# First layer's attention: one maximum over both maps, exponentials read from the PSUM bank, undivided maps joined, outputs by query

## The reference, cut to what matters

```python
def diff_attend(q, k, v, lam):
    s = jnp.einsum('bqhmd,bkhmd->bhmqk', q, k).astype(jnp.float32) * ATTN_SCALE
    p = jax.nn.softmax(s, axis=-1)
    w = (p[:, :, 0] - lam * p[:, :, 1]).astype(v.dtype)
    return jnp.einsum('bhqk,bkhe->bqhe', w, v)
...
def finish(o):
    B, T = o.shape[:2]
    o = rms_norm(o, subln_g) * (1.0 - lam_init)
    return o.reshape(B, T, D_MODEL) @ w_o
```

## Time and profile before

| | us |
|---|---|
| median of 3 runs | 2743.91 |
| lowest and highest run | 2741.31, 2743.94 |
| span of the profiled execution | 2737.2 |
| median less span | 6.7 |

### The profile page before, as it was taken

How to read it: one execution, slowest core, us unless ns; L and a number is a source line. 1 busy time by engine, 2 the same in 40 slices (tenths; PEclk the granted TensorE clock), 3 DMA queues, 4 the chain that set the end, 5 groups by cost and what they waited for, 6 DMA issues and landing times.

```text
span 2737.2 us, 44768 instructions
## 1 busy us (share of the span) xinstructions
PE 2592.4 (95%) x18413; PEld 2330.1 (85%) x18413; DVE 1729.9 (63%) x3255; ACT 1260.2 (46%) x2246; POOL 174.2 (6%) x211
## 2 busy tenths in 40 slices
PE   6999989999989989999999999999999999999998
PEld 4676567888868679999999879899999998798998
DVE  4665946454565566677654877676676558776764
ACT  3444634223255554454444455554544444555543
POOL 1000000000034320000000010000000000100001
PEclk8999999999989999999999999999999999999999
DMA  8655522322325325456555324466765553244653
GB/s 258 209 175 185 186 92 78 104 96 93 100 78 120 88 79 170 166 166 178 165 174 171 123 85 151 129 177 169 201 182 162 171 180 109 85 158 128 175 167 122
DMA packets 515818, 397.02 MB, mean 145 GB/s; under 512 B 26024, under 2 KB 491184, under 8 KB 515616
## 3 DMA queue, kind: packets, MB, share of 16 engines
q1 hardware_dynamic: 512816, 388.02, 46.6%
q0 software_dynamic: 2080, 3.53, 1.0%
q10 hardware_dynamic: 720, 2.62, 0.3%
HBM read 393.08 MB, written 1.05 MB: 144 GB/s over the span
## 4 chain that ended last, share of the span: by engine, by line
PE 81%; DVE 12%; ACT 3%; issue 2%; DMA 1%; POOL 1%; SPq 0%; DVEq 0%; ACTq 0%
PE pv L747 42%; PE pa L747 30%; PE pv L712 4%; DVE Wl L1848 3%; PE pa L712 3%; ACT Wh L1362 1%; PE pa L871 1%; DMA ring<-in_w_mod_dram 1%; PE pa L717 1%; DVE Lb L2000 1%; POOL Pb L2490 1%; DVE T L1921 0%; DVE HTl L1855 0%; DVE T L1920 0%; DVE Pb L2013 0%
## 5 line engine op out<-in xcount | busy, mean ns | idle before, releaser
L1848 DVE TENSOR_TENSOR Wl<-ring,Wh 128x1024 fp32r<-128x1024 f32 (+4 forms) x688 | 760.7, 1147 | 320.2 <-ACT Wh L1362 317.3
L1362 ACT ACTIVATE Wh<-ring 128x1024 fp32r<-128x1024 f32 (+4 forms) x688 | 647.9, 990 | 451.1 <-PE pv L747 446.3
L747 PE MATMUL pa<-HTl,Wh 128*128 128x256 f32 (+2 forms) x1648 | 535.7, 325 | 41.7 <-DVE HTl L1940 23.9
L747 PE MATMUL pv<-HTl,Wh 128*128 128x256 f32 (+1 forms) x1872 | 546.8, 292 | 17.2 <-DVE Wl L1848 5.5
L747 PE MATMUL pv<-HTh,Wl 128*128 128x256 f32 (+1 forms) x1872 | 538.5, 288 | 0.0
L747 PE MATMUL pv<-HTh,Wh 128*128 128x256 f32 (+1 forms) x1872 | 538.0, 287 | 0.0
L747 PE MATMUL pa<-HTh,Wl 128*128 128x256 f32 (+2 forms) x1648 | 521.2, 316 | 0.0
L747 PE MATMUL pa<-HTh,Wh 128*128 128x256 f32 (+2 forms) x1648 | 520.7, 316 | 0.0
L747 PEld LDWEIGHTS pv<-HTl,Wh 128*128 128x128 f32 x1872 | 359.8, 192 | 32.5 <-issue 8.3
L747 PEld LDWEIGHTS pa<-HTl,Wh 128*128 128x128 f32 (+1 forms) x1648 | 320.3, 194 | 77.1 <-issue 43.6
L747 PEld LDWEIGHTS pv<-HTh,Wl 128*128 128x128 f32 x1872 | 360.2, 192 | 2.9 <-issue 0.2
(11 more groups left out here) (237 smaller groups left out, 3836.4 us busy)
## 6 DMA issues: line engine op xcount, KB each, us to landing
ring<-in_ffn_w_gu_dram SPq DMA_DIRECT2D x176, 512.0 KB, 5.1
ring<-in_w_mlp_dram SPq DMA_DIRECT2D x64, 1024.0 KB, 5.3
ring<-in_w_in_dram SPq DMA_DIRECT2D x54, 1024.0 KB, 5.0
ring<-in_w_mod_dram SPq DMA_DIRECT2D x48, 1024.0 KB, 5.9
ring<-in_ffn_w_down_dram SPq DMA_DIRECT2D x64, 704.0 KB, 4.7
ring<-in_a_w_qkv_dram SPq DMA_DIRECT2D x12, 1024.0 KB, 5.3
ring<-in_b_w_qkv_dram SPq DMA_DIRECT2D x12, 1024.0 KB, 5.2
ring<-in_w_out_dram SPq DMA_DIRECT2D x8, 1024.0 KB, 5.1
```

The costliest lines, as they stand in the source:

```text
L747: m = nc.tensor.matmul(o, lhsT=x, rhs=y, start=first and j == 0, stop=last and j == 2)
L1362: ins = nc.scalar.activation(Wh[rows, p % SPLIT, a:b], ring[rows, i % RING, a:b], ACT.Copy)
L1848: ins = v.tensor_tensor(Wl[rows, p % SPLIT, a:b], ring[rows, i % RING, a:b], Wh[rows, p % SPLIT, a:b].bitcast(F32), ALU.subtract)
```

## The change

The first layer's loop becomes a function of its own on PE, ACT and DVE.

- Scores: the two maps of a unit lie in two adjacent banks (`pairs_`). One `tensor_reduce` on DVE takes the negated maxima of both (`nm`, two numbers a row); ACT reads the exponentials straight from the banks, and no copy to `Lb` is made. The banks come free when ACT is done with them.
- Join: with row sums l1 and l2, DVE forms c = -lambda l1 / l2 from two operations on one number a row, then e1 + c e2 in one pass. The pass that scaled the first map is gone; the outputs are too large by l1.
- Outputs: the transposed map is now the stationary operand, so that queries lie on the partitions; they use one fixed bank (`O_BANK`) and `A` rotates over two. ACT takes the mean square of each unit by a Square over 128 columns with a sum. Mean, root and Newton step then work on 4 numbers a row for each head, the epsilon times l1 squared.
- POOL multiplies the head's 128 by 512 outputs by their roots; PE transposes them (4 transposes, `OT`); ACT writes `HTh` from the bank with the gain, and DVE writes `HTl` from it.

```diff
-        pv = [ctx.enter_context(nc.psum_tensor(f"pv{i}", [P, 512], F32)) for i in range(BANKS)]
+        pairs_ = [ctx.enter_context(nc.psum_tensor(f"pv{i}", [P, 2, 512], F32)) for i in range(BANKS // 2)]
+        pv = [pairs_[i // 2][:, i % 2, :] for i in range(BANKS)]
+        O_BANK = pa[BANKS - 2]
...
+            def diff_attention(tag, todo, behind):
+                A.width = 2
+                V.even()
...
+                def outputs_turned(i):
+                    h = last_unit(i, 9)
+                    if h is not None:
+                        pe.wait_ge(on_ready, h + 1)
+                        if A.taken():
+                            pe.wait_ge(a_free, A.taken())
+                        b = A.take((tag, "OT", h))
+                        for t in range(4):
+                            turn(b[:, t * P:(t + 1) * P], Oa[:, h, t * P:(t + 1) * P], a_full if t == 3 else None)
...
+                        h, t, n = todo[i]
+                        for m in range(2):
+                            r = slice(m * HEAD, (m + 1) * HEAD)
                             if V.taken():
                                 pe.wait_ge(v_free, V.taken())
-                            b = V.take((tag, "S", i, m))
+                            mm(V.take((tag, "S", i, m))[:, 0:n], Qa[r, h, t * P:(t + 1) * P], Ka[r, h, 0:n], True, True, v_full)
+                            V.emptied_otherwise((tag, "S", i, m))
...
+                    if i >= 3:
+                        u = i - 3
+                        h, t, n = todo[u]
+                        pe.wait_ge(a_free, A.nth((tag, "T", u)))
+                        if u:
+                            pe.wait_ge(o_free, u)
+                        for k in range(n // P):
+                            mm(O_BANK[:, 0:P], PT[:, u % 2, k * P:(k + 1) * P], Va[:, k, h * P:(h + 1) * P],
+                               k == 0, k == n // P - 1, o_full if k == n // P - 1 else None)
+                    outputs_turned(i)
+                behind(len(todo) + 2)
...
+                def rest_turned():
+                    for i in range(len(todo) + 3, HEAD_NORM_STEPS + 3):
+                        outputs_turned(i)
+                return rest_turned
...
                     src = ht(ALL)
-                    def last_sums(k):
+                    def head_done(k):
                         if k == 4:
-                            for step_ in range(len(todo) + 3, HEAD_NORM_STEPS):
-                                head_sums(step_)
+                            rest_turned()
...
+            def diff_attention(tag, todo, also):
+                for i in range(HEAD_NORM_STEPS + 3):
+                    if i < len(todo):
+                        h, t, n = todo[i]
+                        act.wait_ge(mx_ready, i + 1)
+                        for m in range(2):
+                            nc.scalar.activation(Pb[:, i % 3 * 2 + m, 0:n], V.taken_at((tag, "S", i, m))[:, 0:n], ACT.Exp,
+                                                 bias=nm[:, i % 2, m:m + 1], scale=1.0,
+                                                 accum_out=lsum[:, h % 3, m, t:t + 1]).then_inc(v_free, 1)
...
+                    if 0 <= i - 2 < len(todo):
+                        u = i - 2
+                        n = todo[u][2]
+                        if u >= 1 and last_unit(i - 1, 9) is not None:
+                            act.wait_ge(a_free, A.nth((tag, "OT", last_unit(i - 1, 9))))
+                        copy((tag, "T", u), PT[:, u % 2, 0:n], lambda b: b[:, 0:n])
+                    if 0 <= i - 4 < len(todo):
+                        u = i - 4
+                        h, t, _ = todo[u]
+                        act.wait_ge(o_free, u + 1)
+                        if u >= 2:
+                            act.wait_ge(os_ready, u - 1)
+                        nc.scalar.activation(SQ[:, u % 2, 0:P], Oa[:, h, t * P:(t + 1) * P], ACT.Square,
+                                             accum_out=osum[:, h % 3, t:t + 1]).then_inc(os_ready, 1)
+                    h = last_unit(i, 6)
+                    if h is not None:
+                        act.wait_ge(om_ready, h + 1)
+                        x = oroot[:, h % 2, :]
+                        nc.scalar.activation(x, omean[:, h % 2, :], ACT.Ln).then_inc(log_ready, 1)
+                        act.wait_ge(log_ready, seen.more(log_ready))
+                        nc.scalar.activation(x, x, ACT.Exp, scale=-0.5).then_inc(or_ready, 1)
+                    h = last_unit(i, 9)
+                    if h is not None:
+                        act.wait_ge(a_full, A.nth((tag, "OT", h)))
+                        b = A.bank((tag, "OT", h))
+                        nc.scalar.activation(HTh[:, h, :], b[:, 0:512], ACT.Copy, scale=gq[:, 4:5]).then_inc(oh_ready, 1)
...
+            def diff_attention(tag, todo, also):
+                for i in range(HEAD_NORM_STEPS + 3):
+                    if i < len(todo):
+                        n = todo[i][2]
+                        dve.wait_ge(v_full, V.nth((tag, "S", i, 1)))
+                        at = V.order[V.where[(tag, "S", i, 0)]]
+                        v.tensor_reduce(nm[:, i % 2, :], pairs_[at // 2][:, :, 0:n], axis=AXIS.X, op=ALU.max,
+                                        negate=True).then_inc(mx_ready, 1)
+                    if 0 <= i - 1 < len(todo):
+                        u = i - 1
+                        h, t, n = todo[u]
+                        dve.wait_ge(v_free, V.nth((tag, "S", u, 1)))
+                        l1, l2, c = lsum[:, h % 3, 0, t:t + 1], lsum[:, h % 3, 1, t:t + 1], rr[:, u % 3, 1:2]
+                        step(v.reciprocal(rr[:, u % 3, 0:1], l2))
+                        step(v.scalar_tensor_tensor(c, l1, lamt[:, 5:6], rr[:, u % 3, 0:1], ALU.mult, ALU.mult))
+                        p0 = Pb[:, u % 3 * 2, 0:n]
+                        v.scalar_tensor_tensor(p0, Pb[:, u % 3 * 2 + 1, 0:n], c, p0, ALU.mult, ALU.add).then_inc(pn_ready, 1)
+                    h = last_unit(i, 10)
+                    if h is not None:
+                        dve.wait_ge(oh_ready, h + 1)
+                        b = A.taken_at((tag, "OT", h))
+                        v.scalar_tensor_tensor(HTl[:, h, :], b[:, 0:512], gq[:, 4:5], HTh[:, h, :].bitcast(F32),
+                                               ALU.mult, ALU.subtract).then_inc(a_free, 1)
+                    if 0 <= i - 3 < len(todo):
+                        u = i - 3
+                        h, t, _ = todo[u]
+                        dve.wait_ge(o_full, u + 1)
+                        v.tensor_copy(Oa[:, h, t * P:(t + 1) * P], O_BANK[:, 0:P]).then_inc(o_free, 1)
+                    h = last_unit(i, 5)
+                    if h is not None:
+                        l1 = lsum[:, h % 3, 0, :]
+                        if h:
+                            dve.wait_ge(rn_ready, h)
+                        step(v.scalar_tensor_tensor(otmp[:, :], l1, EPS, l1, ALU.mult, ALU.mult))
+                        dve.wait_ge(os_ready, 4 * h + 4)
+                        v.scalar_tensor_tensor(omean[:, h % 2, :], osum[:, h % 3, :], 1.0 / P, otmp[:, :],
+                                               ALU.mult, ALU.add).then_inc(om_ready, 1)
+                    h = last_unit(i, 7)
+                    if h is not None:
+                        dve.wait_ge(or_ready, h + 1)
+                        x, r = omean[:, h % 2, :], oroot[:, h % 2, :]
+                        step(v.scalar_tensor_tensor(otmp[:, :], r, -0.5, r, ALU.mult, ALU.mult))
+                        step(v.tensor_tensor(otmp[:, :], otmp[:, :], x, ALU.mult))
+                        v.scalar_tensor_tensor(r, otmp[:, :], 1.5, r, ALU.add, ALU.mult).then_inc(rn_ready, 1)
+                    also(i)
...
-                        if maps == 1:
-                            v.tensor_scalar(p0, p0, rr[:, u % 3, 0:1], None, ALU.mult).then_inc(pn_ready, 1)
-                        else:
-                            step(v.tensor_tensor(rr[:, u % 3, 1:2], rr[:, u % 3, 1:2], lamt[:, 5:6], ALU.mult))
-                            step(v.tensor_scalar(p0, p0, rr[:, u % 3, 0:1], None, ALU.mult))
-                            v.scalar_tensor_tensor(p0, Pb[:, u % 3 * 2 + 1, 0:n], rr[:, u % 3, 1:2], p0,
-                                                   ALU.mult, ALU.add).then_inc(pn_ready, 1)
...
-                        h = head_norm(step_, 10)
-                        if h is not None:
-                            r = RQ[:, h % 2, :]
-                            dve.wait_ge(a_free, A.nth(("os", i, h)))
-                            newton(r, XQ[:, h % 2, :], NT)
-                            v.scalar_tensor_tensor(TMP[:, h % 2, :], Oa[:, h, :], gq[:, 4:5], r, ALU.mult, ALU.mult)\
-                             .then_inc(t_ready, 1)
-                        h = head_norm(step_, 12)
-                        if h is not None:
-                            rest(HTh[:, h, :], HTl[:, h, :], TMP[:, h % 2, :])
...
+            for h in range(DA_HEADS):
```

(5 more changed lines are left out.)

## The result

The changed kernel takes 2723.22 us (median of 4 runs, 2721.71 to 2725.89), the kernel before, run beside it, 2742.61 (2739.70 to 2743.94). The ratio is 0.9936, 95% interval 0.9924 to 0.9949: 17.5 us faster (14.0 to 20.8); the difference of the two medians, 19.4, lies in this interval.

The account below looks back on a forecast made before the run. DVE was taken to bound the loop at 14.29 us a head, with PE next at 12.04. Loop -13 plus tail +2.2 gave -10.8 from 2743.9, so 2733 us, range 2727 to 2742.

Parts of the forecast that it names:

- DVE, the maximum: Attention loop: one maximum over both banks takes 1.22 us for 1024 columns, 0.69 for 512, 3.82 a head.
- DVE's total: Attention loop: DVE's work falls from 13.28 to 9.29 us a head, under 80% busy, and stops being the bound.
- One wait stays ... its path is as long as before: Attention loop: PE's outputs still wait 0.66 us a head for ACT's copy of the transposed map, making 12.04 a head.
- PE is the bound there already: First 2.75 heads: PE sets the 11.3 us a head, so they gain only half a microsecond in all.
- The last 0.56 head at 2.25 a head: Loop's end, up to the last output matmul: gains 2.25 us a head like the five heads before it.
- The tail: Projection behind the loop: late hand-overs for heads 6 and 7 give back 2.2 us, bounds +1.2 to +4.0.
- No waits remain: Rival, loop and tail: PE never waits and ACT's additions hide, -16 + 1.2, 2729 us; 13%.
- PE's shown busy time is real: Rival, loop: PE's work is 12.7 us a head, so the loop gains 9, 2737 us; 17%.
- POOL stops DVE's join: Rival, loop: POOL's multiplications hold back joins PE needs, losing 9 of the 13 us, 2742, no change; 10%.
- Twice as dear: Rival, loop: the maximum costs double and DVE stays the bound at 14.1 us a head, +9, 2753 us; 6%.
- DMA: Attention stage: weight transfers would need 235 GB/s if the stage were 13 us shorter, and stay hidden.

Follow-up runs that it names:

- the run with the wide norm: Changed kernel with three 512-wide DVE passes over scratch added in one piece behind each head's Newton step: 2739.85 us, ratio 1.0003.
- both edits of the tail: Changed kernel with head 6's outputs turned between projection heads 0 and 1, and first weight block split one step earlier: 2714.14 and 2713.14 us.
- the earlier turning alone: Changed kernel with head 6's outputs turned between projection heads 0 and 1 instead of 3 and 4: 2712.59 and 2718.35 us.

## Why the prediction was right in direction and wrong in size

- *DVE, the maximum:* 1.22 and 0.69 forecast, 1.225 and 0.682 measured. The two copies it replaced took 2 x 0.686 and 2 x 0.419 a unit, so it is no dearer than they were. The Trainium skill's page "VectorE: DVE Perf Modes", section "Rules for kernel authors", advises to restructure around this reduction, which spoke against the change; the trace is against that advice here. Its one element a cycle is borne out (1.07 us for 1024 columns by that page's figure, an estimate, against 1.225 with the fixed cost).
- *DVE's total:* 9.29 a head forecast, 9.76 measured; the sum left the operations on single numbers as they were, and the one that forms c takes 0.27 where the multiplication by lambda took 0.16. That DVE stops being the bound was right; its share is 84% and not under 80%, since its work fell less and the period further than forecast.
- *PE, "One wait stays ... its path is as long as before":* **this step failed.** I took the row of PE waiting for ACT's copy as the latency of a path that the change leaves alone, and did not follow the chain. In the kernel before it reads, in one head:

```profile
283.93 0.75 DVE TMP L2123
...
285.06 1.09 ACT Pb L1458 x4
286.15 0.52 ACT SQ L1536
286.67 0.52 ACT HTh L1368
287.19 0.49 ACT PT L1431
...
287.72 2.22 PE pv L712 x12
```

DVE's norm holds back the exponentials (ACT is idle for 3.12 us ahead of them), and between them and the copy ACT does two more passes of the norm, its Square and its rounding. All eight waits of the earlier trace rows stand behind such passes of ACT: five behind these two, three behind the three passes for mean and root. The change takes away DVE's part, and ACT's norm now stands behind the copy, so the path became shorter in two places and the wait vanished. The run with the three wide passes puts DVE's part back without ACT's: ACT is idle for 3.39 us again, but the outputs wait for the copy for 1.0 us over five heads and not 3.3. The run with the maximum taken twice shows that DVE's lateness alone can make some of it. How the 3.3 divide between the two is not shown. Five heads were forecast at 12.04 and took 11.61: no wait for the copy, some 0.5 a head for the remainder's bank and a modulation copy (2.3 + 0.2 in that stretch), and 11.1 of PE's own work against 11.38 by distances of starts. That explains 2.2 of the 6.5 us by which the loop was missed; the next two points have the other 4.3.
- *"PE is the bound there already", for the first 2.75 heads:* wrong. Eleven steps in 31.1 us looked like PE's pace, but DVE was busy for 26.11 of the first 28.75 and all of PE's 2.3 us of waits there were for joins. Gain 2.23, not 0.5.
- *The last 0.56 head at 2.25 a head:* wrong in kind. A share of a head was priced by length, but it held a whole norm (DVE's four passes in step 30) and PE waits of 4.4 us. Gain 3.80, not 1.25. In both pieces single joins came late, while the forecast priced DVE by its total per head. The runs show that most of a step's piece is paid when it stands in one place (13.2 of 16.7 us) and most is hidden when it is spread (2.7 of 12.3). By these runs the norm in one step was the dearest part of the old loop: a piece of the same length, put back alone, returns 13.2 of the 19.45, the scaling 5.3. That is from the edits one at a time; the old copies were not put back.
- *The tail:* +2.2 forecast within +1.2 to +4.0, +3.31 measured. The mechanism was right. What it lacked was POOL beside the subtraction (+0.84 on DVE's 2.36) and more time at the lower clock (335.4 to 342.3 and 349.1 to 352.5 us, 10.2 in all, against 6.8 in the tail before): the 24 matmuls of heads 0 to 3 took 8.25 and not 7.21.
- *The rivals:* "No waits remain" (13%) was nearest, and still 6 us short, for the two pieces of loop above. "PE's shown busy time is real" had 12.7 of PE's work a head; it is 55.50 / 5 = 11.1. "POOL stops DVE's join" hardly happened in the loop: the maximum beside POOL keeps its 0.68, POOL takes 1.04, and of the operations behind only the one that forms c is longer, 0.43 and not 0.22, once a head. The overlap showed where the forecast had not put it, in the tail and in the run with the wide norm. The page "SBUF — State Buffer" of the Trainium skill, section "Who interferes with whom", has passes with two SBUF inputs contend with POOL's reads and this reduction never on trn2; both agree with these rows. "Twice as dear" would have ended at no change, not at 2753, by the run with the maximum taken twice. In the earlier trace rows the 0.43 and the 0.84 belong to two different passes; the one of 0.84 takes 0.43 elsewhere in that trace, so the reading stands.
- *DMA:* hidden, as forecast. The loop ran at 243 GB/s and PE waited for no transfer in it; the forecast's 235 is 22.10 MB over 93 us, which gives 238.

## What to carry to other kernels

In a loop whose engines hand work to each other every step, price an edit by the step in which it stands and not by an engine's total per round: here most of a piece in one step was passed on, and most of the same work spread over three steps was hidden. A wait in a profile names the last engine of a chain; before keeping it in a forecast, follow the chain through every pass in that engine's queue and ask which of them the change takes away. When a step is made short and moved to another engine, look at the ends of the loop too, where its new hand-overs have no cover: here the tail lost 3.3 us to them, and moving a few instructions made the stage 7 to 9 us shorter.

## What the runs showed that I had not expected

Behind the stage, where the kernels are the same, the two profiled executions of the kernel with both edits of the tail differ: 2712.8 - 379.77 = 2333.0 us and 2708.8 - 381.59 = 2327.2, from the start of the matmuls that sum the squares to the end of each span. The changed kernel has 2722.2 - 389.16 = 2333.0 there, the earlier turning alone 2327.4 and 2327.5 in its two, so the difference does not go with the kernel. It goes with the granted clock: 0.98 on average behind the stage in the two executions of 2333.0, 0.99 in the three others. It differs in single stretches, such as this one, in the first execution and then, over the same work, in the second:

```profile
774.00:800.00 26.00, 21.06 (x124) 19.32 (x125) 24.32 (x32) 14.67 (x34) 16.86 (x21) 0.87 0.46 130
```

```profile
775.80:801.80 26.00, 20.63 (x134) 18.55 (x135) 24.61 (x32) 15.84 (x37) 17.82 (x20) 1.00 0.46 128
```

The timed runs of the earlier turning alone show the same: four at a mean clock of 0.983 or 0.984 took 2710.8 to 2712.7 us, five at 0.979 or 0.980 took 2717.3 to 2719.8. Why the clock falls there in one execution and not in the other is not shown. The difference is as large as the gains compared in the tail, so these rest on the stage in the traces as well as on medians.

ACT's exponentials of 512 columns take 0.683 us from the PSUM bank, against 0.712 from SBUF before: reading the bank made them no longer.
